# Expert weights loaded as 2 MB pairs with 16 KB per partition, in place of 1 MB loads with rows of 8 and 4 KB

## What is computed

```
def moe_ffn(h, w_router, b_router, w_mlp1, b_mlp1, w_mlp2, b_mlp2):
    logits = (hf @ w_router + b_router).astype(jnp.float32)
    top_val, top_idx = lax.top_k(logits, TOP_K)
    top_w = jax.nn.softmax(top_val, axis=-1).astype(h.dtype)
    ...
    def expert_block(args):
        xblk, e = args
        hm = xblk @ w_mlp1[e] + b_mlp1[e]
        gate, up = hm[:, :D_EXPERT], hm[:, D_EXPERT:]
        gate = jnp.minimum(gate, SWIGLU_LIMIT)
        up = jnp.clip(up, -SWIGLU_LIMIT, SWIGLU_LIMIT)
        act = gate * jax.nn.sigmoid(SWIGLU_ALPHA * gate) * (up + 1)
        return act @ w_mlp2[e] + b_mlp2[e]
    ...
x = x + token_mixer(rmsnorm(x, g_mix[l]), ...)
x = x + moe_ffn(rmsnorm(x, g_ffn[l]), ...)
return rmsnorm(x, g_final)
```

## Time and profile before

| what | value |
|---|---|
| three timed runs | 1300.25, 1307.12, 1304.65 us (median 1304.65) |
| span of the profiled execution | 1303.6 us (the page gives no other time of that execution) |
| PE busy | 1182.3 us, 91% of the span |
| DVE, ACT, POOL busy | 364.2, 193.1, 19.9 us |
| bytes over the DMA queues | 445.18 MB, mean 342 GB/s |
| chain that ended last | PE 40%, DMA 37%, SP's queue 16% |
| mean granted clock of TensorE | 0.984 |

### The profile page before, as it was taken

One profiled execution on the slowest core, in us unless ns is written; L12 is line 12 of the kernel. 1 busy time (PEld: TensorE's weight loads), 2 busy tenths in 40 slices (PEclk: granted clock), 3 DMA queues, 4 the chain that ended last, 5 costly groups with the idle time before them and its releaser, 6 DMA issues.

```text
span 1303.6 us, 18034 instructions
## 1 busy us (share of the span) xinstructions
PE 1182.3 (91%) x6734; PEld 578.6 (44%) x6734; DVE 364.2 (28%) x1018; ACT 193.1 (15%) x362; POOL 19.9 (2%) x32
## 2 busy tenths in 40 slices
PE   5999999998799999989998988888899989998885
PEld 5888888887433333333333333333333333333331
DVE  2515788121412221222121111111122212111112
ACT  1212344001111110111011100100111011001001
POOL 0001111000000000000000000000000000000000
PEclk9999999999699999999999999999999999999998
DMA  9944322654099999999999999999999999999994
GB/s 283 281 142 117 128 97 97 230 217 171 29 417 417 417 417 417 417 417 418 417 418 418 418 418 418 418 418 417 417 417 418 418 418 418 418 418 417 418 417 178
DMA packets 113351, 445.18 MB, mean 342 GB/s; under 512 B 9731, under 2 KB 46947, under 8 KB 80515
## 3 DMA queue, kind: packets, MB, share of 16 engines
q1 hardware_dynamic: 109408, 441.48, 85.0%
q10 hardware_dynamic: 3907, 3.21, 0.9%
HBM read 443.61 MB, written 1.05 MB: 341 GB/s over the span
## 4 chain that ended last, share of the span: by engine, by line
PE 40%; DMA 37%; SPq 16%; issue 2%; DVE 2%; ACT 1%; ACTq 1%; DVEq 0%; POOL 0%; POOLq 0%
DMA ring<-in_w_mlp_dram 37%; SPq L328 16%; PE bank L433 14%; PE bank L629 14%; PE bank L436 5%; PE bank L624 1%; PE bank L611 1%; PE bank L562 1%; PE bank L552 1%; PE bank L698 1%; PE bank L524 1%; PE bank L416 1%; PE bank L663 0%; PE bank L591 0%; PE bank L515 0%
## 5 line engine op out<-in xcount | busy, mean ns | idle before, releaser
L629 PE MATMUL bank<-ring,arena 128*64 128x512 f32 x3072 | 702.7, 600 | 63.7 <-DMA ring<-in_w_mlp_dram 63.6
L629 PEld LDWEIGHTS bank<-ring,arena 128*64 128x64 f32 x3072 | 203.0, 137 | 515.3 <-issue 324.2
L1245 DVE TENSOR_TENSOR arena<-bank,b1T 128x256 f32<-128x256 f32 x128 | 53.8, 420 | 624.3 <-PE bank L663 621.9
L433 PE MATMUL bank<-hT,ring 128*128 128x256 f32 x576 | 128.3, 384 | 0.8 <-DVE hT L995 0.8
L433 PEld LDWEIGHTS bank<-hT,ring 128*128 128x128 f32 x576 | 110.9, 193 | 16.6 <-DVE hT L995 1.2
L436 PE MATMUL bank<-ring,hT 128*128 128x256 f32 x320 | 72.1, 386 | 2.2 <-DVE hT L1156 2.2
L906 ACT ACTIVATE arena<-bank 128x512 f32<-128x512 f32 x32 | 19.1, 597 | 362.4 <-PE bank L629 362.3
L436 PEld LDWEIGHTS bank<-ring,hT 128*128 128x128 f32 x320 | 61.5, 194 | 11.1 <-DVE hT L1156 2.6
L624 PE MATMUL bank<-arena 64*128 64x512 f32 x264 | 65.6, 615 | 0.8 <-ACT arena L916 0.8
L611 PEld LDWEIGHTS bank<-slotP,hb 128*128 128x128 bf16 x1536 | 47.7, 99 | 27.1 <-issue 23.5
L611 PE MATMUL bank<-slotP,hb 128*128 128x64 bf16 x1536 | 51.5, 195 | 3.1 <-DVE arena L1229 3.1
(11 more groups left out here) (204 smaller groups left out, 634.3 us busy)
## 6 DMA issues: line engine op xcount, KB each, us to landing
ring<-in_w_mlp_dram SPq DMA_DIRECT2D x384, 1024.0 KB, 22.1
ring<-in_w_in_dram SPq DMA_DIRECT2D x24, 1024.0 KB, 10.3
ring<-in_w_br_attn_dram SPq DMA_DIRECT2D x4, 1024.0 KB, 4.9
ring<-in_w_br_ssm_dram SPq DMA_DIRECT2D x4, 1024.0 KB, 5.0
ring<-in_w_out_dram SPq DMA_DIRECT2D x4, 1024.0 KB, 5.0
xres<-in_x_dram ACTq DMA_DIRECT2D x1, 1024.0 KB, 4.9
out_dram<-hN SPq DMA_DIRECT2D x2, 512.0 KB, 2.7
cst<-shape_constants_dram ACTq DMA_DIRECT2D x1, 736.0 KB, 6.4
```

The source lines that it names most:

```text
L433: last = nc.tensor.matmul(o, w[:, k, a * P:(a + 1) * P], rhs[:, k, :], start=(k == 0), stop=(k == KD - 1))
L629: return nc.tensor.matmul(bank[b][side * CAP:(side + 1) * CAP, :], tokens, w, start=start, stop=stop, skip_group_check=True)
L1245: step(V.tensor_tensor(o.rearrange("p (m s) -> p m s", m=4), bank[b][:, half].rearrange("p (m s) -> p m s", m=4), bias[:, m0:m0 + 4].unsqu ...
```

## The change

Every expert load becomes 2 MB, two neighbouring slots at once, with 16 KB per partition that are one run in memory: for `w_mlp1` two neighbouring rows (four loads, load a being rows 256a to 256a+255, partition p holding rows 256a+2p and 256a+2p+1), for `w_mlp2` four neighbouring rows (two loads). An expert has six loads, the ring eight pairs, and a pair is freed when both its units are used. What is multiplied with the weights follows that row order: tokens and router weights hold row 256a + 2p + j in block 2a + j (DVE writes `hN` through a strided read), the activation holds row 512a + 4p + i at place 2i + a (ACT reads PSUM with a step of 4 elements into `hs`), the biases are transposed from strided columns, and `g_ffn` is loaded a second time as 4 x 256 and transposed in two more PE instructions.

```
+PAIRS = RING // 2
+PAIR_ORDER = (7, 3, 4, 0, 6, 5, 1, 2)
+EXP_PAIRS = EXP_UNITS // 2
...
         def moe_slot(u):
-            return SLOTS[u % RING]
+            return 2 * pair_at(u // 2) + u % 2
...
         def moe_full(eng, i, u):
-            s = moe_slot(u)
-            eng.wait_ge(slot_full[s], 16 * (mix_loads(s) + u // RING + 1) + i * (16 * BODY * EXP_UNITS // RING))
+            g = u // 2
+            eng.wait_ge(pair_full[pair_at(g)], 16 * (g // PAIRS + 1) + i * (16 * BODY * EXP_PAIRS // PAIRS))
...
-        w1v = w_mlp1[0].rearrange("e (k p) n -> e p k n", p=P)
-        w2v = w_mlp2[0].rearrange("e (k p) n -> e p k n", p=P)
-        w2h = w_mlp2[0].rearrange("e (a j p) n -> e j p a n", a=2, p=P)
+        w1v = w_mlp1[0].rearrange("e (a p j) n -> e a p (j n)", p=P, j=2)
+        w2v = w_mlp2[0].rearrange("e (a p j) n -> e a p (j n)", p=P, j=4)
+
+        def pair_src(e, r):
+
+            if r < KD // 2:
+                return w1v[bass.ds(e, 1), r, :, :].rearrange("a p n -> (a p) n")
+            return w2v[bass.ds(e, 1), r - KD // 2, :, :].rearrange("a p n -> (a p) n")
+
+        def pair_dst(p):
+            return ring[:, 2 * p:2 * p + 2, :].rearrange("p s n -> p (s n)")
...
+            def load_moe(i, g):
+                p = pair_at(g)
+                sp.dma_start(pair_dst(p), pair_src(i * BODY + g // EXP_PAIRS, g % EXP_PAIRS)).then_inc(pair_full[p], 16)
...
-            sp.wait_ge(row_in, 16 * 5)
+            sp.wait_ge(row_in, 16 * 6)
...
-            for u in range(BODY * EXP_UNITS):
-                if u < RING:
-                    first_free(moe_slot(u))
+            for g in range(BODY * EXP_PAIRS):
+                if g < PAIRS:
+                    first_free(pair_at(g))
                 else:
-                    unit_used(sp, 0, u - RING)
-                load_moe(0, u)
+                    unit_used(sp, 0, 2 * (g - PAIRS) + 1)
+                load_moe(0, g)
...
+            for j in range(2):
+                nc.tensor.transpose(bank[6][:, R_GFFN:R_GFFN + KD].rearrange("p (a j) -> p j a", j=2)[:, j, :], gfr[:, j, :], ident[0:4, 0:4])
...
+            act.dma_start(arena[0:4, 0:256], g_ffn[0].rearrange("(a c) -> a c", a=4)).then_inc(row_in, 16)
...
-                nc.scalar.activation(hs[:, 0:512], bank[0][:, :], ACT.Copy).then_inc(hs_ready, 1)
+                nc.scalar.activation(hs[:, 0:512].rearrange("q (i p) -> q i p", i=4),
+                                     bank[0][:, :].rearrange("q (p i) -> q i p", i=4), ACT.Copy).then_inc(hs_ready, 1)
...
-                V.tensor_scalar(hN[:, t, :], xres[:, t, :], stat[:, 20 + t:21 + t], None, ALU.mult).then_inc(h2_ready, 1)
+                V.tensor_scalar(hN[:, t, :].rearrange("p (a j q) -> p a j q", j=2, q=P),
+                                xres[:, t, :].rearrange("p (a q j) -> p a j q", j=2, q=P),
+                                stat[:, 20 + t:21 + t], None, ALU.mult).then_inc(h2_ready, 1)
```

More of the change, by code:

```diff
@@ L199, in encoder_layer @@
         iota = cst[:, C_IOTA:C_IOTA + CAP]
-        slot_full = [sem(f"slot_full{i}") for i in range(RING)]
+        slot_full = [sem(f"slot_full{i}") for i in range(RING_MIX)]
+        pair_full = [sem(f"pair_full{i}") for i in range(PAIRS)]
         unit_done = sem("unit_done")
@@ L397, in _ @@
             pe.wait_ge(c_in, 16)
-            pe.wait_ge(row_in, 16 * 5)
+            pe.wait_ge(row_in, 16 * 6)
             pe.wait_ge(dsk_ready, 1)
             nc.tensor.transpose(bank[6][:, 0:N_ROWS], prm[0:N_ROWS, :], ident[0:N_ROWS, 0:N_ROWS])
+            for j in range(2):
+                nc.tensor.transpose(bank[6][:, R_GFFN:R_GFFN + KD].rearrange("p (a j) -> p j a", j=2)[:, j, :], gfr[:, j, :], ident[0:4, 0:4])
             nc.tensor.transpose(bank[6][:, N_ROWS:N_ROWS + 8], dske[:, :], ident[0:8, 0:8]).then_inc(prm_ready, 1)
             pe.wait_ge(b1_in, 16)
-            for m in range(16):
-                o = (m // KD) * KD + spot(m % KD)
-                last = nc.tensor.transpose(bank[7][:, o * NE:(o + 1) * NE], b1raw[:, m * P:(m + 1) * P],
-                                           ident[0:NE, 0:NE])
+            for b in range(2):
+                for a in range(2):
+                    for i in range(4):
+                        o = b * KD + 2 * i + a
+                        last = nc.tensor.transpose(bank[7][:, o * NE:(o + 1) * NE], b1v[:, b, a, i, :], ident[0:NE, 0:NE])
             last.then_inc(prm_ready, 1)
@@ L651, in down_unit @@
                 w = ring[:, moe_slot(u), :]
-                for a in range(2):
+                for ii in range(2):
                     for side, unit_half in ((0, left_done), (1, right_done)):
-                        o = a * D + side * 512
-                        mm = half_product(2, side, act32[:, 2 * j + a, :], w[:, o:o + 512],
-                                          j == 0 and a == 0, j == 3 and a == 1)
-                        if a == 1:
+                        o = ii * D + side * 512
+                        mm = half_product(2, side, act32[:, 2 * (2 * (j % 2) + ii) + j // 2, :], w[:, o:o + 512],
+                                          j == 0 and ii == 0, j == 3 and ii == 1)
+                        if ii == 1:
                             mm.then_inc(unit_half, 1)
@@ L1239, in activations, with side @@
                 bias = b1T[:, bass.ds(e, 1), :].rearrange("p a m -> p (a m)")
-                half = slice(4 * h * CAP, 4 * (h + 1) * CAP)
-                g_, u_, s_ = ga[:, half], ub[:, half], sg[:, half]
+                def side(x):
+                    return x.rearrange("p (i a s) -> p i a s", i=4, a=2)[:, :, h, :]
+                g_, u_, s_ = side(ga), side(ub), side(sg)
                 for o, b in ((g_, 0), (u_, 1)):
-                    m0 = b * KD + 4 * h
+                    bias_h = bias[:, b * KD:(b + 1) * KD].rearrange("p (i a) -> p i a", a=2)[:, :, h:h + 1]
                     dve.wait_ge(t_psum, 2 * e + (b + 1))
-                    step(V.tensor_tensor(o.rearrange("p (m s) -> p m s", m=4), bank[b][:, half].rearrange("p (m s) -> p m s", m=4),
-                                         bias[:, m0:m0 + 4].unsqueeze(2).to_broadcast([P, 4, CAP]), ALU.add))
+                    step(V.tensor_tensor(o, side(bank[b][:, :]), bias_h.to_broadcast([P, 4, CAP]), ALU.add))
                     if b == 0:
```

84 lines of the change are left out of this document (34 added, 50 removed).

## The result

| | before | changed |
|---|---|---|
| timed runs | 1300.25 to 1307.12 us, 4 runs | 1284.34 to 1287.15 us, 4 runs |
| median | 1305.75 us | 1285.98 us |
| span of the profiled execution | 1303.6 us | 1282.5 us (time 1284.34) |
| ratio | | 0.9854, 95% interval 0.9832 to 0.9876 |

The changed kernel takes 1.5% less: the medians differ by 19.8 us, and the interval leaves 1 out. The forecast was 1288.7, in a range of 1272 to 1302.

A forecast was written before the change was run, and what follows sets the result against it. The prediction took the expert weights' DMA stream, not PE, to bound the kernel. -20.0 + 1.8 + 1.8 + 0.5 = -15.9 us took the span from 1303.6 to 1287.7, time 1288.7 us, range 1272 to 1302.

The forecast's parts named there:

- The step from span to time: Whole kernel: the timed median lies 1.05 us above the profiled span, added to the predicted span of 1287.7.
- A megabyte: Expert weight stream: 16 KB rows cut each of 364 units from 2.511 to 2.456 us, -20.0 us.
- Start of the stream: First expert load after the ring's fill: waits until PE has used two units instead of one, +1.8 us.
- The stream just holds: First expert: the pairs freed by its up units last the DMA until the next release, 0 us.
- fourth rival: Expert stage: pairs open holes in the stream; 0.5 us per expert gives 1304 us, 1 us gives 1320; chance 0.08.
- End: After the last up landing: PE has two units left instead of one, +1.8 us; the last down pair stays hidden.
- Filling: Ring's first filling: the last pair and the later wait of pair 7 are hidden before PE reads, 0 us.
- ACT's extra DMA: Kernel start: one more DMA on ACT's queue ahead of its first work, +0.5 us.
- DVE's strided read: Writes of `hN` before the expert stage: reading every second element costs 0 to +1.5 us, taken as 0.
- the line that ends at 8 KB: Expert stream: rows beyond 8 KB give nothing, only W2 gains, 1301.5 us; chance 0.14.
- the slope alone: Expert stream: the packet overhead goes nearly entirely, 434 GB/s, 1274 us; chance 0.10.
- a dearer 16 KB packet: Expert stream: a 16 KB packet costs more than two of 8 KB, breaking even at 625 ns; slower; chance 0.08.

The follow-up runs named there:

- eighth kernel: The changed kernel again, unaltered, for a second trace: 1285.21 us, ratio 0.9841.
- tenth: The kernel before again, unaltered, for a second trace: 1303.75 us in one execution.
- fourth kernel: Changed kernel with the first pair after the fill and the last up pair each loaded as two 1 MB halves: 1286.09 us, ratio 0.9857.
- sixth: Changed kernel with 4 MB loads of 32 KB rows for `w_mlp1` from the third expert to the last but one: 1287.11 us, ratio 0.9864.
- second kernel: Changed kernel with its row order and its DVE and ACT forms, but 1 MB loads of 8 KB rows in single slots: 1295.23 us, ratio 0.9925.
- first experiment: Kernel before with loads joined to 2 MB pairs and freed in pairs, rows still 8 and 4 KB: 1307.54 us, ratio 1.0024.
- ninth kernel: Changed kernel with 4 MB loads for `w_mlp1` only from the fifth expert on, and the last up pair in halves: 1284.56 us, ratio 0.9855.

## Why the prediction was right, step by step

The forecast's mechanism and its sign held. The span fell by 21.1 us where 15.9 had been summed; the two terms that make the difference are the first and the last here. The medians differ by 19.8 us. The step from span to time, +1.05, was too small: in the changed kernel's profiled execution the time is 1284.34 - 1282.5 = 1.84 us above the span. That error of 0.8 us lowered the forecast and so brought it nearer to the measured time, which is luck.

- **A megabyte, -20.0 forecast, -22.7 measured** in the first pair of profiles, 895.90 - 919.31 = -23.4 in the second (the eighth kernel, whose rows are below, and the tenth). Over 364 units the first is 0.062 us per MB; I had 0.055, from 2.511 to 2.456. The line was right and its constant slightly off: the stream runs at 428 and 429, not 427. This term was mis-sized by 2.7 us, and it is all of the gain, as the prediction said.
- **Start of the stream, +1.8.** Measured +1.83, and +2.00 in the second pair of profiles. The fourth kernel showed what the prediction did not: this cost is no separate term that could be won back, because the stream that starts earlier runs dry earlier and lost more than it had won.
- **The stream just holds, 0.** Right, and as tight as summed: DMA share 1.01 in 362 to 382. Starting 1.6 us earlier (fourth kernel) or releasing in quads (sixth) opens the hole that the fourth rival spoke of.
- **End, +1.8.** Measured +1.67, and +1.64 in the second pair of profiles; 16 records after the last up landing, and the last down pair hidden.
- **Filling, 0.** The stage still enters with a full ring: 64 records without a wait. The later release of pair 7 shows nowhere.
- **ACT's extra DMA, +0.5.** It took 0.49; the table load moved from 8.95 to 9.22, the first product of the mixer from 19.55 to 19.83: +0.3. SP's first load moved by 0.55, inside the 0 to 1 left for it, and nothing waited for that. **The two small transposes, 0**: the table load alone moved by 0.27 and PE's first product by 0.28, so nothing is left for them.
- **DVE's strided read, 0 to +1.5.** 751 ns against 749: 0. **ACT's read of PSUM with a step of 4**: a mean of 597 ns on L906, as in the page of before: 0. **The halves in pieces of 64**: a mean of 420 ns for DVE's first step of a half, as in the page of before: 0. The second kernel, which has all three forms and no pairs, confirms it as a whole.
- **What no term had: when the expert stage starts**, -1.93 in the first pair of profiles and +1.07 in the second (351.43 against 350.36). It is no effect of the change, by the section on the hardware.

The timeline of the second profile of the changed kernel (the eighth of the experiments), for the second pair:

```profile
19.84 4.53 PE L429 MATMUL bank<-hT,ring 128*128 128x256 f32 x11 [0.78 <-DVE hT L998]
...
351.43 15.61 PE L625 MATMUL bank<-ring,arena 128*64 128x512 f32 x64
...
356.86 10.62 SPq L331 DMA_DIRECT2D ring<-in_w_mlp_dram  x4
...
1252.76 3.65 PE L625 MATMUL bank<-ring,arena 128*64 128x512 f32 x16 [1.24 <-DMA ring<-in_w_mlp_dram]
```

Its pieces against the tenth kernel's are +1.07, +2.00, -23.41 and +1.64, together -18.7, which is 1283.3 - 1302.0. Without the stage's start the two pairs agree at -19.2 and -19.8, where the forecast has -16.4 (the 0.5 of ACT's DMA left out, since it lies ahead of that start). The difference is the rate and little else.

The rivals: the line that ends at 8 KB (1301.5) is refuted by the 428 of the changed kernel and the 432 of 32 KB rows; the slope alone (434 GB/s) was not reached by either; a dearer 16 KB packet needed more than 625 ns and it took 16 x 16384 / 428 = 612; and holes did not open. The Trainium skill ("DMA: Bandwidth & Descriptors", section "Why small descriptors are slow (HBM only)") puts the overhead at about 3 cycles a packet and 32 bytes of metadata; an estimate from these figures gives 0.8% for the step from 8 to 16 KB, and the trace differs: 422 to 428 GB/s is 1.4%, with loads of 2 MB that the first experiment shows to give nothing by themselves. The same section's rule that packetization is worth it only up to 256 B is about putting consecutive descriptors into one packet; the prediction read it as speaking against long rows, which it does not, and no run here tries what it is about. The Trainium skill ("Perfetto Trace Analysis", section "DMA Optimizations") says that batching small transfers into larger ones, for example 2 KB into 4 or 8 KB, can improve the throughput dramatically. Taken as the row length, these runs agree, since 2 to 8 KB in loads of 1 MB raised the rate from 387 to 422, and they show that two more doublings still raise it, by 6 and 4 GB/s.

## What to carry to other kernels

In a stream that is never out of work, with loads of 1 to 4 MB and several of them queued, what counts is the contiguous run per partition, not the size of a load: fit a line through two row lengths in stretches where one alone is in flight, and it tells the rate at others. The price of a longer row is the coarser grain of its buffer, paid once where the stream starts and once where it ends, so it is worth it for a long stream and not a short one, and each doubling doubles the price while the gain shrinks. Before winning back such an end cost, ask which release the stream waits for next; if that one doesn't move, an earlier start is only an earlier hole. And where coarse loads are kept away from the ends, look for their cost inside the stream: the sixth kernel paid it 27 us into the stage.

## What the runs showed of the hardware

The moment at which TensorE begins to work at its higher level differs between executions of the same kernel. The two profiles of the kernel before have 11 products of the mixer in 4.85 us and 20 in 4.58 us (the tenth kernel), both from 19.6 us on; the two of the changed kernel have 19 in 4.37 and 11 in 4.53. That is 0.41 to 0.44 us a product against 0.23, near the factor of two between the levels. The clock's column reads 1.00 from 19.9 to 24 us in all four, but the trace's record of the clock only begins with the rise: at about 24.1 and 18.7 us in the two profiles of the kernel before, at 18.9 and 23.7 us in those of the changed kernel, which is what the counts say. The delay is still there at the writes of `hN`, at 323.4 and 321.2 us in the one kernel, 321.4 and 323.4 us in the other. At the second place the clock's own column tells: in 350 to 355 us it was 0.50, the lower level throughout, in the first profile of the kernel before, 0.65 in the changed kernel's, so part of it at the higher, and 0.50 in the ninth kernel's, which was at 0.65 even in 355 to 358. In the 10 us ahead of that PE had been busy for 7.26, 9.19 and 8.22 us, at a clock of 0.50; in the eighth kernel's profile it had been busy for only 6.92 us and the clock was 0.60 already, then 0.66, so PE's busy time alone does not order these cases. Together the two places go with starts of the expert stage between 350.36 and 353.47 us over twelve profiles, and nothing behind it takes that back. So a single pair of profiles carries an error of 2 to 3 us that has nothing to do with the edit: compare pieces of the span, as above, and not spans.

The 32 KB kernel also showed the clock falling in the steady part without harm: a mean of 0.98 in 604 to 1200 us, where it was 1.00 with pairs, and a rate of 432 all the same, since PE is not what is waited for.
